# Sparse attention in another order: the last query block by turns with the second, then the third with the first

## What is computed

```python
def nsa_attention(h, w_in, w_out, rel_bias, k_cmp, v_cmp, k_slc, v_slc, k_win, v_win):
    proj = h @ w_in
    q = proj[..., :H * d].reshape(B, T, G, R, d)          # G = 4 groups of R = 4 heads, d = 64
    gates = sigmoid(proj[..., H * d:]).reshape(B, T, G, R, 3)
    # for every block of queries:
    s_c = einsum('bqgrd,bgnd->bgrqn', qi, k_cmp) * scale       # 31 compressed keys
    p_c = softmax(where(valid_c, s_c, NEG)) * valid_c
    o_c = einsum('bgrqn,bgnd->bqgrd', p_c, v_cmp)
    s_s = ... * scale + bias;  o_s = softmax(s_s) @ vs     # selected blocks: top 16 of 8, so all causal keys
    s_w = ... * scale + bias;  o_w = softmax(s_w) @ vw     # window of 512, so all causal keys too
    o = gi[..., 0:1] * o_c + gi[..., 1:2] * o_s + gi[..., 2:3] * o_w
    return o.reshape(B, T, H * d) @ w_out
```

## Time and profile before

| | us |
|---|---|
| median of 3 runs (1904.43 to 1906.19) | 1905.62 |
| the profiled execution: its time | 1905.81 |
| the profiled execution: its span | 1904.0 |
| PE busy in the span | 1863.4 (98%) |
| DVE / ACT / POOL busy | 1151.8 / 867.5 / 79.3 |
| first transposes of sparse attention | at 754.57 |
| output projection (tile 29) starts | at 906.56 |

### The profile page before, as it was taken

The page is one execution under the profiler, slowest core; times in us unless marked ns, Lnnn a source line. Parts: engine busy times, 40 slices in busy tenths (PEclk is TensorE's granted clock), DMA queues, the critical chain, the costliest instruction groups (busy, mean ns, idle before and its releaser), DMA issues.

```text
span 1904.0 us, 23960 instructions
## 1 busy us (share of the span) xinstructions
PE 1863.4 (98%) x9006; PEld 1510.8 (79%) x9007; DVE 1151.8 (60%) x2050; ACT 867.5 (46%) x1527; POOL 79.3 (4%) x133
## 2 busy tenths in 40 slices
PE   7999999999999999999999999999999999999999
PEld 6777788888888887666788888888878888887887
DVE  7677786565567487766454334346744554867664
ACT  4247643232223574878242313135354434668553
POOL 0000000000000000455000000000000000000000
PEclk9999999999999999999999999999999999999999
DMA  9741255555455231000422232322211231232021
GB/s 373 299 188 45 92 197 206 192 178 213 181 190 185 89 113 65 1 1 1 145 89 89 90 108 88 99 99 89 89 67 67 89 138 67 89 133 89 1 100 66
DMA packets 42567, 223.81 MB, mean 118 GB/s; under 512 B 4541, under 2 KB 5309, under 8 KB 23919
## 3 DMA queue, kind: packets, MB, share of 16 engines
q1 hardware_dynamic: 42098, 222.37, 32.5%
q10 hardware_dynamic: 380, 0.28, 0.1%
HBM read 219.45 MB, written 3.19 MB: 117 GB/s over the span
## 4 chain that ended last, share of the span: by engine, by line
PE 87%; DVE 5%; ACT 4%; DMA 2%; issue 1%; POOL 1%; SPq 0%; DVEq 0%; ACTq 0%
PE bank L440 24%; PE bank L442 24%; PE bank L441 24%; PE bank L1948 2%; DMA raw<-wts_d 1%; PE bank L1987 1%; PE bank L908 1%; POOL pB L2046 1%; PE bank L2600 1%; PE bank L928 1%; PE bank L3299 1%; DVE wL L417 1%; DVE tmp L654 1%; ACT wH L412 1%; PE bank L917 1%
## 5 line engine op out<-in xcount | busy, mean ns | idle before, releaser
L440 PE MATMUL bank<-hH,wH 128*128 128x512 f32 x1208 | 472.9, 391 | 2.7 <-issue 1.4
L442 PE MATMUL bank<-hH,wL 128*128 128x512 f32 x1208 | 470.3, 389 | 0.0
L441 PE MATMUL bank<-hL,wH 128*128 128x512 f32 x1208 | 470.1, 389 | 0.0
L1193 ACT ACTIVATE wH<-raw 128x2048 fp32r<-128x2048 f32 x64 | 122.7, 1917 | 463.7 <-PE bank L442 463.7
L1238 DVE TENSOR_TENSOR wL<-raw,wH 128x2048 fp32r<-128x2048 f32 x64 | 146.6, 2291 | 269.0 <-ACT wH L1193 269.0
L440 PEld LDWEIGHTS bank<-hH,wH 128*128 128x128 f32 x1208 | 226.8, 188 | 51.7 <-issue 2.1
L442 PEld LDWEIGHTS bank<-hH,wL 128*128 128x128 f32 x1208 | 226.7, 188 | 47.4
L441 PEld LDWEIGHTS bank<-hL,wH 128*128 128x128 f32 x1208 | 226.8, 188 | 47.1 <-issue 0.5
L417 DVE TENSOR_TENSOR wL<-raw,wH 128x2048 fp32r<-128x2048 f32 x71 | 162.7, 2291 | 129.4 <-ACT wH L412 129.2
L412 ACT ACTIVATE wH<-raw 128x2048 fp32r<-128x2048 f32 x76 | 145.4, 1913 | 158.6 <-PE bank L442 116.5
L442 PE MATMUL bank<-aH,wL 128*128 128x512 f32 x512 | 199.2, 389 | 0.0
(11 more groups left out here) (415 smaller groups left out, 2696.2 us busy)
## 6 DMA issues: line engine op xcount, KB each, us to landing
raw<-wts_d SPq DMA_DIRECT2D x140, 1024.0 KB, 5.0
adab<-ada_d SPq DMA_DIRECT2D x72, 512.0 KB, 5.9
adac<-ada_d SPq DMA_DIRECT2D x24, 512.0 KB, 6.5
adaP<-ada_d SPq DMA_DIRECT2D x3, 2048.0 KB, 26.3
bt<-bias_rows SPq DMA_DIRECT2D x4, 1024.0 KB, 9.5
x<-x_d SPq DMA_DIRECT2D x2, 1024.0 KB, 8.7
adaP<-ada_d SPq DMA_DIRECT2D x2, 1024.0 KB, 12.9
peF<-ple_d SPq DMA_DIRECT2D x2, 1024.0 KB, 5.8
```

The source lines that it names most:

```text
L440: pe.matmul(o, l[0], r[0], start=start, stop=False)
L441: pe.matmul(o, l[0], r[1], start=False, stop=False)
L442: return pe.matmul(o, l[1], r[0], start=False, stop=stop)
L1193: act.activation(wH[:, n % 2, :], raw[:, n % 2, :], ACT.Copy).then_inc(w_hi, 1)
```

## The change

It changes five things. The order of groups: blocks 0 and 1 swap places, so block 3 goes by turns with block 1 (the second), then block 2 (the third) with block 0 (the first). `ORDER` and `BEGIN`, which place the compressed branch, follow. The special buffer for the last set goes: the last set is now (0, 3) and has the third buffer by the general rule. ACT rounds the first half of the output projection's weights in step UN - 5 = 83 and not in step 81, and waits there for the scores of 86 units and not 84, since group 2's queries (whose place it takes) are now read up to unit 85.

```diff
-        GROUPS = [(3, 0), (3, 1), (0, 0), (3, 2), (0, 1), (3, 3), (0, 2), (0, 3),
-                  (2, 0), (2, 1), (1, 0), (2, 2), (1, 1), (2, 3), (1, 2), (1, 3)]
-        ORDER = (3, 0, 2, 1)
+        GROUPS = [(3, 0), (3, 1), (1, 0), (3, 2), (1, 1), (3, 3), (1, 2), (1, 3),
+                  (2, 0), (2, 1), (0, 0), (2, 2), (0, 1), (2, 3), (0, 2), (0, 3)]
+        ORDER = (3, 1, 2, 0)
...
-        BEGIN = [4, 15, FIRST[2] - 2, FIRST[1] - 6]
+        BEGIN = [4, 15, FIRST[2] - 2, FIRST[0] - 6]
...
-            if (i, g) == (1, 3):
-                PT.append(3)
-            elif i == 0 and g != 2:
+            if i == 0 and g != 2:
...
-                if t == UN - 7:
-                    act.wait_ge(n_mm, UN - 4)
+                if t == UN - 5:
+                    act.wait_ge(n_mm, UN - 2)
                     hi(act, HALF0["b_out"])
```

## The result

The changed kernel is slower: median 1909.89 us of 7 runs (1907.60 to 1914.85) against 1904.43 of 7 runs of the kernel before on the same chip (1902.37 to 1906.19). The ratio is 1.0033, with a 95% interval of 1.0023 to 1.0043, which is some 6 us. Five later runs on another occasion gave 1.0041 (1.0027 to 1.0055).

A forecast was written before the change was run, and what follows sets the result against it. PE, busy for 98% of the span, bounds the kernel, so only its idle time could change. Terms -0.5 + 2.4 - 0.2 = +1.7 us on the profiled 1905.81 gave 1907.5, as median 1907.3; range 1904.0 to 1912.0.

The forecast's parts named there:

- the likeliest case, no change that can be measured: Whole kernel: time within about 0.2% (3.8 us) of before, chance 0.55.
- First half, forecast -0.5: Block 3 by turns with block 1: waits for POOL sum to 4.6 us against 5.1 before, -0.5 us.
- The waits counted for units 21 and 41: First half, units behind sets of values: 0.45 us at 21 (block 3), 1.15 at 41 (block 1).
- Second half, forecast +2.4: Block 2 by turns with block 0: waits sum to 8.9 us against 6.5, with 2.5 each at 65, 75, 85.
- the reason given: Second unit of each block 0 pair: its exps stand on ACT behind a copy (unit 65's behind 62's), 2.5 us each.
- The end, forecast -0.2: From unit 82's transposes to tile 29: PE idle 3.1 us against 3.27 before, -0.2 us.
- The walk through the queues: End of the stage, engine by engine from unit 82's transposes: PE fed until 7.3 us, tile 29 able to start at 12.9.
- The first rival: End, unit 84 to tile 29: clock falls to 1.2 GHz for a while, 3.4 us lost, 1910.7 us; chance 0.15.
- The second, the rounding shown whole: End: rounding before unit 86's exps shows whole, +1.9 us and some 0.6 for DVE's queue, 1909.8 us; chance 0.15.
- this rival's sign: Start of tile 29: later than 910 at full clock would show that the end is worse.
- The third, block 0 hidden: Second half loses 2.8 us instead of gaining 2.4, 1902.1 us; sign: waits of 65 and 75 under 1.5; chance 0.12.
- The fourth, that all cancels: Both halves: what leaves one comes back in the other, 1905.6 us; chance 0.20.

The follow-up runs named there:

- parity experiment: Changed kernel with DVE copying the transposes of block 1's odd units instead of its even ones: 1913.53 us, ratio 1.0040 to the kernel before.
- second of the three other orders: Changed kernel with block 0 in one run between groups 1 and 2 of block 2, rounding back at UN - 7: 1903.70 us, ratio 1.0001.
- the fills: Changed kernel with dummy identity products on PE ahead of units 64, 65, 74, 75 and 84 to 87: 1909.37 us, ratio 1.0023 to the kernel before.
- both remedies: Changed kernel with the first half of `lo_part` earlier on DVE and dummy identity products in PE's waits: 1907.48 us, ratio 1.0016 to the kernel before.
- before, `lo_part` early: Kernel before with the second half of `lo_part` ahead of DVE's copy of unit 86: 1904.84 us, ratio 0.9999.
- the early `lo_part`: Changed kernel with the first half of `lo_part` on DVE ahead of unit 86's reciprocal: 1907.37 us, ratio 1.0014 to the kernel before.
- third of the three other orders: Changed kernel with block 0's first group alone, its other three in one run, block 2's last group at the end, rounding at UN - 7: 1905.75 us, ratio 1.0009.

## Why the prediction came out as it did

The number lay 2.6 us below the result and the result within the range, but the likeliest case, no change that can be measured, was not the one that came: the kernel is 0.33% slower, to which the prediction gave 0.33. The direction of the sum was right, +1.7 us, and its size too small: the rise over the kernel before on the same chip is 5.5 us by the medians and some 6 by the ratio. That the number lies only 2.6 us off is in part luck, since it was put on a base of 1905.62 and the kernel before had 1904.43 when it ran again. By its steps, in PE's idle time, which unlike PEld's waits adds up to the distance that was measured. The first half and the second, before and then in the second profile of the changed kernel; the second half ends ahead of unit 84's wait in the old order and behind unit 85's in the new:

```profile
781.13:834.89 53.76, 49.36 (x365) 36.80 (x366) 36.56 (x162) 41.06 (x134) 28.94 (x52) 1.00 0.00 1
834.89:899.10 64.21, 60.30 (x422) 42.97 (x420) 44.25 (x188) 53.11 (x163) 33.67 (x55) 1.00 0.00 1
...
780.44:844.21 63.77, 59.63 (x422) 42.80 (x423) 41.41 (x166) 48.34 (x141) 31.99 (x51) 1.00 0.01 1
844.21:903.59 59.38, 51.66 (x370) 38.32 (x368) 39.76 (x189) 46.71 (x153) 31.08 (x55) 0.97 0.01 2
```

**First half, forecast -0.5: -0.3.** PE is idle for 4.4 us before and 4.1 after; its waits for POOL are 3.2 us in both. The waits counted for units 21 and 41 came (0.92 and 1.22 where 0.45 and 1.15 were counted), and that of the earlier trace rows went. What the count left out was the second chain, over DVE's copy of block 1's even units, which the parity experiment showed: waits at 20, 32 and 44. The second of the three other orders confirms that this half is neutral.

**Second half, forecast +2.4: about +3.8.** PE is idle for 3.9 us before and 7.7 after. A pair of block 0 costs what was forecast, 2.5 us: at units 64 and 65 the distances are 2.16 and 1.80 where 0.68 and 0.80 would be the plain pace. But the reason given was wrong in part. The 2.5 fall on both units, and what holds the second is for the most part POOL, busy with eight scalings in a row, not ACT's copy ahead of the exps. PEld's waits came close to the forecast too: 9.3 us from 868.8 to unit 85, where 8.9 were counted. What was mis-sized is what goes away. The 6.5 us of the earlier trace rows were PEld's waits, of which PE itself lost only 3.3; of the 9.3 that came PE loses 6.8. Before, in the stretch of the earlier trace rows, and after:

```profile
PE bank L1987 <- POOL pB L2046: 3.3, 6, 0.9
...
PE bank L1985 <- POOL pB L2044: 6.8, 7, 1.5
```

**The end, forecast -0.2: +1.6 at the full clock.** The walk through the queues was good up to POOL: unit 85 at 4.71 us behind unit 82's transposes (forecast 4.7), the last scalings begun at 6.63 (7.05), the rounding between the exps of 85 and 86. Then POOL needed 5.58 us for what the walk counted at 3.46, since DVE's two halves of `lo_part` were beside it. With the fills, at the full clock, tile 29 starts at 14.3 instead of 12.9, and PE's own products leave 2.0 us free ahead of unit 86 and 2.1 ahead of unit 87, against the 2.6 that PE was idle in the old end (899.10 to 906.56, with the 4.86 busy of the earlier trace rows). With both remedies it starts at 13.3. This is the term that was mis-sized most: it priced POOL's scalings by a row without such a neighbour, though the row of before had it in sight, for POOL's last four scalings of 256 took 3.05 us there and 2.38 by the earlier trace rows.

**The first rival came true beside the forecast, not in its place.** Its condition was that the waits at 84 to 87 lie close together. The clock fell there, but also at 888, between the units of the pair 74, 75. The rival's 3.4 us are about what a run at a mean clock of 0.996 has lost against one at 0.998 (0.002 x 1910 = 3.8 with PE busy throughout). The prediction weighed the old end at 4.86 of 7.40 us busy against it; this did not carry over to a new end with waits of 1.8 and 2.4 us around short transposes. Nor was the old end as safe as one profile made it look: in that of the kernel before with the late rounding the clock was at half from 907.9 to 911.3, just behind the start of tile 29. The Trainium skill, page "TensorE: Matmul & The Clock Gate", Part 4 (PE-mode transpose), that transposes do not count as busy in the same way, spoke for this rival; these traces agree with it but do not isolate transposes, since the fills were products and stood in the gaps.

**The other rivals.** The second, the rounding shown whole, did not come: the walk, which had the exps of unit 86 behind the rounding, held up to POOL, and POOL's longer time covers what came on top. The rounding alone has a ratio of 0.9999 in the old order; in the new one, where POOL stands idle for 1.98 us behind it, it was not tried. Its result, 1909.8, is close to the measured one for another reason. With the fills tile 29 came at 913.67, later than the 910 at full clock that the prediction had named as this rival's sign, so the sign did not tell it from POOL's contention. The third, block 0 hidden, is refuted by the pairs, although its sign too was there: the waits of 65 and 75 are 1.11 and 1.23, under 1.5, because the first unit of each pair took the larger part. The fourth, that all cancels, holds for the first half alone.

The sum at the full clock is then -0.3 + 3.8 + 1.6 = 5.1 us, close to the 4.9 in the profile with fills and to the 4.9 between the means of the runs with fills (1909.50) and of the kernel before (1904.64), which have nearly the same mean clock. The 12 runs of the changed kernel have a mean of 1911.05 us; of the 6.4 us over the kernel before some 1.5 are left for the lower clock, and some 5.6 in the longest run (1914.87 - 1904.4 - 4.9). That the clock takes this share is worked out and not measured by itself: the fills raised the mean clock from 0.996 to 0.998 and shortened the mean time by 1.6 us (1911.05 to 1909.50), by 2.5 if only the five runs on the same chip are taken (1911.95). Still open is why the stretches come in other places, and in other number, from one execution to the next; of 27 runs of the kernel before 5 had 0.997 or less too.

## What to carry to other kernels

When pieces with a long chain on a slow engine are spread out so that each has neighbours, an entry into them can cost its own fill of the chain: some 1.5 us beside the short units of block 2, where one run of them, away from the end of the stage, was cheaper by some 5 us in all; beside the long ones of block 3 it was cheaper by nothing. A wait of PE's weight loads is not yet a wait of PE: before waits are added or taken away in a sum, see how much of them PE itself loses. When a chain's end is priced, look at what the neighbour engine does in the same microseconds, not at the mean duration. And once waits of 1 to 2 us stand close together on PE, count the clock too: it can cost beyond the waits themselves, and it differs from run to run, so take several runs before a profile is believed.

## What the runs showed of the hardware

**DVE's instruction with two inputs from SBUF all but stops POOL.** The scalings beside `lo_part` (raw and wH in, wL out), the time that as many take with none beside them, and the overlap of the two engines (in us):

| kernel | scalings | taken | plain | longer by | overlap with `lo_part` |
|---|---|---|---|---|---|
| changed | 8 of 128 | 5.58 | 3.44 | 2.14 | 2.50 |
| changed, second profile | 8 of 128 | 4.52 | 3.44 | 1.08 | 1.59 |
| before | 4 of 256 | 3.05 | 2.25 | 0.80 | 1.02 |
| before, `lo_part` early | 4 of 256 | 4.11 | 2.25 | 1.86 | 2.22 |
| both remedies | 8 of 128 | 4.51 | 3.44 | 1.07 | 1.26 |
| second of the other orders | 2 of 384 | 3.25 | 1.31 | 1.94 | 2.24 |

The plain 3.44 is the row of the early `lo_part` above. The plain 2.25 and the 3.05 are these two rows of the kernel before, with the `lo_part` beside the latter:

```profile
898.67 2.25 POOL L2046 TENSOR_SCALAR pB<-pB,rs,gate 128x256 f32<-128x256 f32 x4 [2.13 <-DVE rs L2065]
901.19 1.21 DVE L425 TENSOR_TENSOR wL<-raw,wH 128x1024 fp32r<-128x1024 f32 x1
901.38 3.05 POOL L2046 TENSOR_SCALAR pB<-pB,rs,gate 128x256 f32<-128x256 f32 x4 [0.45 <-DVE rs L2065]
```

this is the second profile of the changed kernel, and the last row the second of the other orders, where the two halves of `lo_part` begin at 902.72 and 903.93:

```profile
905.51 4.52 POOL L2044 TENSOR_SCALAR pB<-pB,rs,gate 128x128 f32<-128x128 f32 x8 [1.98 <-DVE rs L2063]
905.90 1.22 DVE L425 TENSOR_TENSOR wL<-raw,wH 128x1024 fp32r<-128x1024 f32 x1
909.66 1.44 DVE L425 TENSOR_TENSOR wL<-raw,wH 128x1024 fp32r<-128x1024 f32 x1
...
902.90 3.25 POOL L2046 TENSOR_SCALAR pB<-pB,rs,gate 128x384 f32<-128x384 f32 x2 [0.31 <-DVE rs L2065]
```

POOL loses 68 to 87% of each overlap. The Trainium skill, page "SBUF — State Buffer", section "Who interferes with whom", says that a DVE instruction with two SBUF inputs contends with a GpSimd instruction that reads SBUF; its section "SBUF: two separate sides" calls this an exclusive lock, in which the later one waits for the whole instruction. The trace agrees for POOL, which loses most of the overlap but not all; DVE's own duration stayed at 1.20 to 1.28 us, with one of 1.44.

**Short gaps can be enough for the lower clock.** In the profile of the changed kernel PE waits for POOL four times from 868.8 to 888.7, none longer than 1.3 us, and between them does transposes, scores and values:

```profile
PE bank L1985 <- POOL pB L2044: 4.2, 4, 1.3
```

At 888.5, ahead of the transposes of unit 75, the clock was granted at half. The four other profiles of this order without fills show a fall at the same place of the work, within 0.4 us of the start of unit 75's transposes (at 886.1, 886.5, 888.3 and 890.0). Identity products of a few tenths of a microsecond in those gaps kept it at 1.00 from 870 to 925 in both profiles that have them, at the price of no time that the runs could show. The gaps alone do not decide, though: in the third of the three other orders four such waits at the same units (1.31, 0.81, 0.98 and 0.78 us) passed at the full clock.
